# High parts of the down products' weights made by a transfer that casts, not by ScalarE

## The reference

```python
h = h + sq_relu_mlp(rms_norm_2(h, mlp_norm_g[layer]), mlp_w_up[layer], mlp_w_down[layer])
# mlp_w_up: 1024 x 4096, mlp_w_down: 4096 x 1024
# hidden = square(relu(u @ w_up));  result = hidden @ w_down
```

## Time and profile before

| | |
|---|---|
| time, median of 3 runs | 1833.34 us (1831.85 to 1833.65) |
| the profiled execution | 1832.36 us, its span 1830.3 us |
| TensorE busy | 1786.5 us, 98% |
| VectorE busy | 1153.7 us, 63% |
| ScalarE busy | 866.5 us, 47% |
| GpSimd busy | 447.4 us, 24% |
| DMA | 149.22 MB, mean 82 GB/s |
| granted TensorE clock | 0.998 of full |

### The profile page before, as it was taken

The page is one execution under the profiler, slowest core; times in us unless marked ns, Lnnn a source line. Parts: engine busy times, 40 slices in busy tenths (PEclk is TensorE's granted clock), DMA queues, the critical chain, the costliest instruction groups (busy, mean ns, idle before and its releaser), DMA issues.

```text
span 1830.3 us, 26599 instructions
## 1 busy us (share of the span) xinstructions
PE 1786.5 (98%) x10528; PEld 1466.9 (80%) x10532; DVE 1153.7 (63%) x1869; ACT 866.5 (47%) x1409; POOL 447.4 (24%) x451
## 2 busy tenths in 40 slices
PE   7999999999999999999999999999999999999997
PEld 6987777766678757677889898988888788989896
DVE  5355555575545688854577585765677656858574
ACT  5236665355435465564345352533444534435253
POOL 0035551011311235551140000005678214000000
PEclk9999999999999999999999999999999999999999
DMA  5221111231012421111232322222222123232322
GB/s 183 95 67 50 55 50 58 81 97 53 24 47 89 136 67 36 35 36 58 81 115 93 115 93 104 84 99 83 87 89 76 50 81 127 82 115 93 106 91 81
DMA packets 44522, 149.22 MB, mean 82 GB/s; under 512 B 6000, under 2 KB 6384, under 8 KB 44400
## 3 DMA queue, kind: packets, MB, share of 16 engines
q1 hardware_dynamic: 44400, 147.53, 24.0%
HBM read 139.64 MB, written 2.10 MB: 77 GB/s over the span
## 4 chain that ended last, share of the span: by engine, by line
PE 86%; DVE 6%; ACT 3%; POOL 2%; issue 2%; DMA 0%; POOLq 0%; SPq 0%; DVEq 0%; ACTq 0%
PE BANK L301 18%; PE BANK L303 18%; PE BANK L302 18%; PE BANK L2382 4%; PE BANK L2383 4%; PE BANK L2380 4%; PE BANK L933 3%; PE BANK L667 2%; PE BANK L1717 1%; PE BANK L1698 1%; PE BANK L1674 1%; PE BANK L990 1%; PE BANK L2713 1%; PE BANK L652 1%; PE BANK L2688 1%
## 5 line engine op out<-in xcount | busy, mean ns | idle before, releaser
L269 ACT ACTIVATE WH<-WRAW 128x1024 fp32r<-128x1024 f32 (+1 forms) x214 | 222.9, 1044 | 341.4 <-PE BANK L303 312.5
L278 DVE TENSOR_TENSOR WL<-WRAW,WH 128x1024 fp32r<-128x1024 f32 (+1 forms) x201 | 258.3, 1286 | 131.2 <-ACT WH L269 130.9
L301 PE MATMUL BANK<-HH,WH 128*128 128x512 f32 x664 | 273.1, 411 | 12.0 <-DVE WL L278 9.8
L303 PE MATMUL BANK<-HL,WH 128*128 128x512 f32 x664 | 260.2, 392 | 0.0
L302 PE MATMUL BANK<-HH,WL 128*128 128x512 f32 x664 | 259.9, 391 | 0.0
L301 PE MATMUL BANK<-HIDH,WH 128*128 128x512 f32 (+1 forms) x520 | 201.4, 387 | 1.6 <-issue 1.5
L302 PE MATMUL BANK<-HIDH,WL 128*128 128x512 f32 (+1 forms) x520 | 200.9, 386 | 0.0
L303 PE MATMUL BANK<-HIDL,WH 128*128 128x512 f32 (+1 forms) x520 | 200.8, 386 | 0.0
L2383 PE MATMUL BANK<-HP,G 128*128 128x256 f32 x672 | 190.5, 283 | 0.0
L2382 PE MATMUL BANK<-HP,G 128*128 128x256 f32 x672 | 190.5, 283 | 0.0
L2380 PE MATMUL BANK<-HP,G 128*128 128x256 f32 x672 | 190.4, 283 | 0.0
(11 more groups left out here) (446 smaller groups left out, 3755.3 us busy)
## 6 DMA issues: line engine op xcount, KB each, us to landing
WRAW<-in_w SPq DMA_DIRECT2D x77, 512.0 KB, 3.5
WRAW<-in_wd SPq DMA_DIRECT2D x64, 512.0 KB, 3.5
RAW<-in_wf SPq DMA_DIRECT2D x32, 512.0 KB, 3.6
WRAW<-in_wu SPq DMA_DIRECT2D x16, 512.0 KB, 3.4
TMP<-in_wf SPq DMA_DIRECT2D x16, 512.0 KB, 3.5
WRAW<-in_w0o SPq DMA_DIRECT2D x8, 512.0 KB, 3.5
WRAW<-in_w1o SPq DMA_DIRECT2D x8, 512.0 KB, 3.4
WRAW<-in_wc SPq DMA_DIRECT2D x8, 512.0 KB, 3.4
```

The source lines that it names most:

```text
L269: e.activation(WH[b % NS][:, 0:n], WRAW[b % NR][:, 0:n], ACT.Copy).then_inc(*inc("s_high", ("high", b)))
L278: e.tensor_tensor(WL[b % NS][:, 0:n], WRAW[b % NR][:, 0:n], WH[b % NS][:, 0:n].bitcast(F32), ALU.subtract).then_inc(*inc("s_low_pool" if p ...
L301: e.matmul(dst, ah, bh, start=first and i == 0, stop=False)
L303: made = e.matmul(dst, ah, bl, start=False, stop=last and i == len(sets) - 1)
```

## The change

The high parts of the 64 down blocks (32 in each MLP) are no longer made by ScalarE from WRAW. GpSimd starts a transfer from the same DRAM array to WH[b % 3]; the source is float32 and the destination float32r, so the transfer casts. The load to WRAW stays, since the low part is made from it. The low part now waits for the load and for the cast, and TensorE waits for the cast's semaphore instead of ScalarE's. GpSimd's transfers stand in `mlp_gpsimd`: the first three behind the low parts and plane_mix of m = 5, 6, 7, all others behind these, in the order of the blocks, each waiting until block b-3 is used.

```diff
+        cast = [b for b, (_, _, _, key) in enumerate(stream) if key[0][0] == "dn"]
+
+        def high_made(b):
+
+            if b in cast:
+                return dma(f"s_high_cast{b % NS}", 1 + sum(a % NS == b % NS for a in cast if a < b))
+            return at("high", b)
...
         def split_high(e, w, b):
-            if b >= len(stream):
+            if b >= len(stream) or b in cast:
                 return
...
+        def cast_high(e, w, b):
+            name, i, n, _ = stream[b]
+            w.wait_ge(*at("used", b - NS))
+            e.dma_start(WH[b % NS][:, 0:n], A[name][i]).then_inc(*dma(f"s_high_cast{b % NS}"))
+
         def split_low(e, w, b, pool):
...
-            w.wait_ge(*at("high", b))
+            if b in cast:
+                w.wait_ge(*dma(f"s_w{b % NR}", b // NR + 1))
+            w.wait_ge(*high_made(b))
...
             def down(c, m, ks):
...
-                w.wait_ge(*at("high", b))
+                w.wait_ge(*high_made(b))
                 w.wait_ge(*at("low", b))
...
                 if m > 3:
                     plane_mix(e, w, L, m - 4)
+                if m > 4:
+                    cast_high(e, w, block[("dn", L, 0), m - 5])
+            for c in range(4):
+                for m in range(8):
+                    if c or m > 2:
+                        cast_high(e, w, block[("dn", L, c), m])
```

## The result

The changed kernel takes 1878.72 us (median of 4 runs, 1876.74 to 1880.46) against 1832.74 (1831.85 to 1833.65) for the kernel before on the same chip: a ratio of 1.0239, 95% interval 1.0217 to 1.0261, 46 us slower. The prediction was 1881 (1866 to 1921). Its profiled execution took 1880.46 us, span 1878.7.

What follows compares the result with a forecast made beforehand. TensorE, busy 98% of the span, was taken to bound the kernel, so relieving ScalarE gives 0; two loops of 23.95 us add 47.9 to 1832.36, making 1880.3, and the median's 1.0 more gives 1881 us (range 1866 to 1921).

Steps and rivals of the forecast that it cites:

- the loop: Passage from up tiles to down products: VectorE, ScalarE and GpSimd steps wait serially on each transfer, costing 23.95 us a layer.
- GpSimd's part: In each round at the passage, GpSimd's low part plus plane_mix, from start until free for the transfer: 5.13 us.
- C: Time from GpSimd and the slot being free until VectorE can start the low part: 5.1 us, range 3.5 to 8.6.
- 8.65 + 3C: TensorE's delay a layer at the passage, through the end of down block 2: 23.95 us at C = 5.1.
- The term for GpSimd's handling: Part of C added to the 3.5 us landing, sized like a GpSimd instruction on 128x512: 1.3 us.
- The estimate of 4.2 for C: Alternative C from the Trainium skill's transfer figures; the sum would be 42.5 us and not 47.9.
- The other 58 blocks cost nothing: Down blocks after the first three of each MLP: casts land in time at C = 5.1, adding 0 us.
- The window: Block 3 of chunks c = 1 to 3, six tight places: no cost unless C exceeds 5.45 us.
- The idle stretches: TensorE idle before down blocks 0, 1 and 2 of c = 0: 9.0, 9.35 and 6.7 us, 25 a layer.
- hidden: First three transfers land ahead of VectorE's need, no loop forms, TensorE's two waits vanish: 1831.7 us; chance 0.05.
- slow transfer: The casting transfer itself is slow, C above 8.6 us; at C = 12 the kernel takes 1986 us; chance 0.11.
- Rival 3: Loop partly hidden: GpSimd issues quickly, C = 3.5, some 2 us a layer given back: 1867.6 us; chance 0.12.

## Why the prediction was right, and where it was off

The time, the place and the loop were right. Three of the sizes in it were not: by its own signs (GpSimd's part shorter than 5.13, C not near 5, plain loads slowed by the casts) it was off in all three. That the median came within 3 us of 1881 is luck, as the sums below show.

**The loop** was right, by its steps and its place: GpSimd free, transfer, low part, evacuation, square, rounding, low part, plane_mix, transfer. Its sum for a layer was 8.65 + 3C = 23.95; the profile has 19.1 and 18.9. Three terms are off:
- *C*, 5.1 forecast, measured 4.10, 3.86 and 3.91 from the start of GpSimd's transfer instruction to VectorE's low part. The term for GpSimd's handling was sized like an elementwise instruction (1.3) and is 0.57 to 0.76, and most of it lies inside the time to landing; the 0.3 for the two semaphores stood in no row. All that comes on top of a landing of 3.5 measured 0.4 to 0.6 us and not 1.6. Three C's too long: 3.4 us.
- *GpSimd's part of the round*, 5.13 forecast. It took 937.78 - 933.71 = 4.07, as plane_mix's first subtraction needed 1.26 and not 2.27. The row of before was taken while VectorE worked (its low part at 921.73 lasts until 923.2); in the loop VectorE stands idle. The same subtraction ahead of the first transfer took 1.28. Three rounds: 3.1 us.
- *TensorE's clock*, not in the sum at all. The ninth matmul of block 2 comes 3.5 us after its first (954.21 to 957.70), where it takes 8 x 0.227 = 1.8: 1.7 us more. Blocks 0 and 1 ran slow too, but into waits.

23.95 - 3.4 - 3.1 + 1.7 = 19.15, and 19.1 was measured. The errors were of both signs.

The estimate of 4.2 for C from the Trainium skill's figures (DMA: Bandwidth & Descriptors, Anatomy of one DMA) was nearer than mine: the trace shows 3.9 to 4.1 in the loop. That page's own fit gives 3.2, below every landing of these transfers (3.6 at the least); the last microsecond, the time to the first byte, had been added to it. The Trainium skill's page on the shared port pair (SBUF — State Buffer, Who interferes with whom) also bears on the second term: it says that a VectorE instruction with two SBUF inputs holds up a GpSimd instruction that reads SBUF. The trace agrees for plane_mix's subtractions, 1.26 and 0.73 with VectorE idle, up to 2.27 and 1.06 beside it. I had quoted the smaller difference and not drawn it into the sum.

**"The other 58 blocks cost nothing"** failed, for 8.9 us. The window was read rightly: block 3 of c = 1 to 3 brought no wait (C was 3.8 to 3.9 there, the bound 5.45). The step that failed is the last sentence, that adds behind a waiting low part come late by 1 us and nothing reads them until the pass. It took C as one number. Block 7's cast stood beside block 7's load and the three fast loads, and its C was up to 7.25; what stands behind it on VectorE is not only adds but the sums for the pass, where VectorE has no room to catch up (shown by the kernel with block 7 on ScalarE and by the one with the low parts later). That the traffic makes block 7's cast slow is read from the rows, the share of 0.98 above all, and was not tested.

**The idle stretches** were forecast at 9.0, 9.35 and 6.7 and were 7.1, 4.3 and 2.1. The first is the loop's shorter start. The others are shorter about half because a round took 11.2 and not 13.5, and half because the slow clock stretched the matmuls in between, which changes no end. The sum over 1881 came out right since 2 x 4.9 us too much for the loop stood against 8.9 too little for the rest. The 1.5 us that arose ahead of the first down block are in no term. The rivals "hidden" and "slow transfer" are out: in the form of the change nothing was hidden, and the cast itself is about as fast as a plain load. Rival 3 had one thing right, that GpSimd issues quickly: by its sum the two loops lose 34.3, by the forecast's 47.9, and they lost 38.0.

**What stays open:** why block 7's cast takes 5 us in some chunks and 7 in others (some tenths of a microsecond between SyncE's and GpSimd's issues may decide; that was not tried). It may also be why the kernels with this loss scatter more (1841 to 1853) than the one without (1832 to 1837).

## What to carry to other kernels

Moving a step to another engine moves it behind that engine's queue. Before the change, follow one round over all in-order queues that it joins: here low part, evacuation, rounding, low part, plane_mix and transfer closed a ring that had been open, and six of 64 transfers made four fifths of the loss. The same transfers one step ahead in the queue cost 0.3 us in each MLP instead of 19. And an engine that is idle half of the time gives nothing back when it is relieved, if the one that sets the end never waits for it.

## What the runs showed of the hardware

TensorE's clock was low behind short idle stretches. Busy time by stretch, changed kernel; the number behind the five engines is the granted clock, 0.50 of 2.4 GHz, the 1.2 GHz level, right behind the idle 7.1 us, full in the stretch of 950 to 954.2, and mixed again behind an idle time of only 2.1 us:
```profile
931.80:936.00 4.20, 4.20 (x10) 3.33 (x11) 0.50 (x1) 1.26 (x2) 2.29 (x2) 0.50 0.41 125
...
950.00:954.20 4.20, 2.12 (x10) 1.44 (x9) 1.31 (x2) 1.14 (x1) 1.06 (x2) 1.00 0.81 224
954.20:958.00 3.80, 3.79 (x10) 2.98 (x11) 2.94 (x3) 0.00 (x0) 0.00 (x0) 0.55 0.98 304
```
At that level matmuls start 0.43 us apart, not 0.23. The mean clock of the run is 0.988, the kernel before has 0.998.

A transfer of 512 KB from GpSimd that rounds float32 to float32r lands after 3.6 us at best, 4.0 in the median and 7.2 at worst, and occupies GpSimd for 0.53 to 0.60 us (0.76 the first time). Beside the casts, SyncE's plain loads of the same size landed after 4.0 us in the median and not 3.5, and the fast loads after 4.4 and 5.0, not 3.6 and 3.5.

A two-input subtraction of GpSimd on 128x512 took 1.26 to 1.28 us with VectorE idle and 2.27 beside VectorE's low part; one on 128x256 took 0.74, and 2.40 beside the low part of HP.
